# Padding the k tiles of hT by 16 bytes in a one-core decoder layer

## The chip, the cores and the metric

The kernel runs on one NeuronCore of one Trainium2 chip. The metric is the device time of one execution in microseconds; lower is better. All numbers below are of the kernel before the change.

## What is computed

One hybrid decoder layer on 256 tokens with a model width of 2048, all in float32:

```python
h = _rms_norm(x, attn_norm_g[l])
proj = h @ w_in[l]
da_q, da_k, da_v, r_q, r_k, r_v, r_g, m_q, gates = _split_cols(proj, IN_SIZES)
o_da = _diff_attention(...)
o_ret = _retention(...)
o_mem = _memory_attention(...)
merged = (sigmoid(g_da) * (o_da @ w_o_da[l])
          + sigmoid(g_ret) * (o_ret @ w_o_ret[l])
          + sigmoid(g_mem) * (o_mem @ w_o_mem[l]))
x = x + merged @ w_out[l]
hf = _rms_norm(x, ffn_norm_g[l])
x = x + (silu(hf @ w_ffn_gate[l]) * (hf @ w_ffn_up[l])) @ w_ffn_down[l]
```

`w_in` is 2048 x 13312, `mem` has 256 tokens and its own 2048 x 2048 weights, `w_ffn_gate` and `w_ffn_up` are 2048 x 5632, `w_ffn_down` is 5632 x 2048. Almost all of the work is matrix products of 256 tokens with these weights.

## The kernel before, in words

**Products.** A product of activations and weights is made of matmuls of 128 x 128 stationary elements with 512 streamed columns. The stationary operand, the one that is loaded into the array ahead of each matmul, is a tile of transposed activations; the streamed operand is a piece of the model's weights. (In the profile "PEld" is the load of the stationary tile and "PE" the matmul; "weights" in this text and in the change's name are the model's weights, which are streamed.) Both are kept as two parts of the type float32r, a high part and the rest, and a product is three matmuls into one PSUM bank: high x high, high x rest, rest x high (`three_passes`, lines 1592 to 1600, and `product`, lines 1688 to 1692). So in each group of three the stationary tile is hi, hi, lo.

**The activations.** `hT_hi` and `hT_lo` (lines 137 and 138) hold the transposed activations: 128 partitions, KD = 16 tiles for the 16 pieces of 128 of the model width, and TOK = 256 tokens in each tile, that is 1024 bytes per partition and tile. A matmul takes one half of a tile (tokens 0 to 127 or 128 to 255, 512 bytes). They hold the normalised x for the input projection and all three branch gates, later the normalised residual for the feed-forward part, and at the end four tiles of the last feed-forward activations. `oT_hi` and `oT_lo` hold other activations in the same form (the memory tokens, the branches' outputs, the merged columns), `aT_hi` and `aT_lo` those of the down projection. `r_cmb`, `p_cmb` and `cmb` hold sums and differences of blocks of hT (`combine`, line 1424; also lines 1066 and 1313): in part of the products, seven block products are made in place of eight, and four of these take a block of hT and three a combined one.

**Places in SBUF.** Tensors are allocated one behind the other. The small constants come first, then a filler of 32 bytes (`align`, line 136), hT_hi, hT_lo, and behind them everything large: `raw`, `w_hi`, `w_lo` (a ring of four pieces of weights, as loaded, high part and rest), the mixers' tensors and, over the same space, the feed-forward part's. The sizes of all these large ones are multiples of 512 bytes per partition.

**Order of the work.** Stages in order of time: the memory's keys and values on oT (8.6 to 96 us), the memory queries on hT (to 140), the plain and the combined part of the input projection on hT (to about 411), the differential attention and the retention with the gates on hT and the output projections on oT (to about 840), the output projection on oT (to 935), the first feed-forward tile on hT (to 973), ten feed-forward steps with gate and up on hT and combined tiles and down on aT (to 1590), and the last down projection on hT (to 1621). Each engine runs its own program, written out by hand in this order. SyncE's queue brings the model's weights in pieces of 512 KB; ScalarE makes the high part of each piece and VectorE the rest; TensorE waits on `lo_done` (or `part_lo` in the feed-forward part) and releases the slot with `pair_used` (or `part_done`). Between the matmuls on weights stand the small ones of the three attentions and groups of transposes (`turn`, line 1622), four to eight at a time.

**What writes and reads hT besides matmuls.** ScalarE writes hT_hi tile by tile from the transposed input (`high_input`, line 535) and later from PSUM (`high_columns`, line 541), VectorE writes hT_lo in the same way (lines 964 and 956), and at the end one operation of each engine writes four tiles (lines 824 and 1422). VectorE adds hT_hi and hT_lo to make the combined tiles (lines 1066, 1313 and 1427).

Of the kernel before, what the change touches and what calls it, by code (L numbers as in the profile page):

```python
# [27 lines left out]
F32R = mybir.dt.float32r  # L28
# [5 lines left out]
P = 128  # L34
D = 2048
TB = 2
TOK = TB * P
NCOL = 512
KD = D // P
# [52 lines left out]
def program(nc, x, mem, positions, w_in, da_q_norm_g, da_k_norm_g, da_lambda_q1, da_lambda_k1,  # L92
# [6 lines left out]
    with ExitStack() as ctx:  # L99
        def sb(name, shape, dt=F32):  # L100
            return ctx.enter_context(nc.sbuf_tensor(name, shape, dt))
# [32 lines left out]
        rden = sb("rden", [P, 4, 2])  # L134
        lrden = sb("lrden", [P, 2, 2])
        sb("align", [P, ALIGN])
        hT_hi = sb("hT_hi", [P, KD, TOK], F32R)
        hT_lo = sb("hT_lo", [P, KD, TOK], F32R)


        with ExitStack() as mixers:
# [1918 lines left out]
```

## Time and profile before

| | |
|---|---|
| median of two runs | 1623.25 us (1622.8 to 1623.7) |
| the profiled execution, its own time | 1622.59 us |
| its span in the trace | 1620.8 us |
| instructions in the trace | 19825 |
| matmuls | 7355 |
| TensorE matmuls busy | 1613.9 us |
| VectorE, ScalarE, GpSimd busy | 1305.7, 915.7, 80.6 us |
| transfers | 341.45 MB, on average 211 GB/s |

The span is what lies between the first and the last record of the trace; the execution's own time is 1.8 us more. A busy TensorE is not TensorE at its peak: matmuls overlap in the pipe, and the trace models their ends. Starts are records, so the distance of two starts is what to look at.

### The profile page before, as it was taken

What the parts mean: (1) busy time and instruction counts of PE and PEld (TensorE: products, weight loads), DVE (VectorE), ACT (ScalarE), POOL (GpSimd) and SP (SyncE); (2) the same over time, 40 slices, a digit from 0 to 9 for tenths busy, and PEclk for the clock granted to TensorE, in tenths of its full rate; (3) what the DMA queues carried; (4) which work ended last, traced back from release to release, by engine and by line L of the source; (5) the groups of instructions that cost most, each with busy time, mean ns of one, the idle gap of its engine ahead of it and who ended that gap; (6) DMA issues with size and microseconds to landing.
All of it is one profiled execution on the core that took longest, in us unless ns stands there. A gap on an engine that the chain in (4) does not pass through costs nothing.

```text
span 1620.8 us, 19825 instructions
## 1 busy us (share of the span) xinstructions
PE 1613.9 (100%) x7355; PEld 1336.1 (82%) x7355; DVE 1305.7 (81%) x1361; ACT 915.7 (56%) x993; POOL 80.6 (5%) x73
## 2 busy tenths in 40 slices
PE   9999999999999999999999999999999999999999
PEld 7888888888888888888888888888888888888887
DVE  5565658898677777787975589999999999999995
ACT  6654555555555544444554455665656655656653
POOL 0000000000011000000000000100100100100101
PEclk9999999999999999999999999999999999999999
DMA  9776555666645555566666746868868868868866
GB/s 351 268 214 194 157 150 177 213 201 196 193 156 168 165 162 172 180 186 202 206 233 192 258 147 210 256 211 254 243 216 245 252 206 251 246 217 240 251 213 177
DMA packets 178013, 341.45 MB, mean 211 GB/s; under 512 B 11792, under 2 KB 16400, under 8 KB 177168
## 3 DMA queue, kind: packets, MB, share of 16 engines
q1 hardware_dynamic: 167056, 319.45, 60.8%
q0 software_dynamic: 10880, 20.97, 7.1%
q8 instruction: 49, 0.80, 0.2%
q14 instruction: 28, 0.23, 0.0%
HBM read 317.31 MB, written 2.10 MB: 197 GB/s over the span
## 4 chain that ended last, share of the span: by engine, by line
PE 85%; issue 11%; DVE 1%; POOL 1%; DMA 1%; ACT 0%; DVEq 0%; ACTq 0%; SPq 0%; POOLq 0%
PE acc L1600 38%; PE at L1692 9%; PE at L1691 9%; PE at L1690 9%; PE acc L1692 5%; PE acc L1690 5%; PE acc L1691 5%; PE at L1600 3%; PE at L1622 2%; POOL rstd L487 1%; PE at L1653 0%; PE at L1670 0%; DMA raw<-in_w_mem_kv 0%; DMA raw<-in_w_in 0%; DVE w_lo L938 0%
## 5 line engine op out<-in xcount | busy, mean ns | idle before, releaser
L938 DVE TENSOR_TENSOR w_lo<-raw,w_hi 128x1024 fp32r<-128x1024 f32 x313 | 378.9, 1223 | 196.0 <-ACT w_hi L514 190.7
L514 ACT ACTIVATE w_hi<-raw 128x1024 fp32r<-128x1024 f32 x313 | 330.6, 1060 | 341.9 <-PE acc L1600 274.0
L1600 PE MATMUL acc<-w_hi,hT_hi 128*128 128x512 f32 x664 | 262.8, 396 | 0.0
L1600 PE MATMUL acc<-w_hi,hT_lo 128*128 128x512 f32 x664 | 258.8, 390 | 0.0
L1600 PE MATMUL acc<-w_lo,hT_hi 128*128 128x512 f32 x664 | 258.6, 390 | 0.0
L866 ACT ACTIVATE f_hi<-sum 128x2048 fp32r<-128x2048 f32 x60 | 115.3, 1922 | 122.0 <-DVE sum L1479 118.8
L1600 PE MATMUL acc<-w_hi,oT_hi 128*128 128x512 f32 x384 | 151.2, 394 | 1.1 <-DVE oT_lo L964 1.1
L1600 PE MATMUL acc<-w_hi,oT_lo 128*128 128x512 f32 x384 | 149.7, 390 | 0.0
L1600 PE MATMUL acc<-w_lo,oT_hi 128*128 128x512 f32 x384 | 149.4, 389 | 0.0
L1445 DVE TENSOR_TENSOR f_raw_rest<-f_raw,f_hi 128x2048 fp32r<-128x2048 f32 x64 | 145.3, 2284 | 4.3 <-ACT f_hi L856 4.3
L1600 PEld LDWEIGHTS acc<-w_hi,hT_hi 128*128 128x128 f32 x664 | 124.7, 188 | 27.4 <-issue 1.3
L1600 PEld LDWEIGHTS acc<-w_hi,hT_lo 128*128 128x128 f32 x664 | 124.6, 188 | 26.6
L1600 PEld LDWEIGHTS acc<-w_lo,hT_hi 128*128 128x128 f32 x664 | 124.8, 188 | 25.0
L1458 DVE TENSOR_TENSOR sum_rest<-sum,f_hi 128x2048 fp32r<-128x2048 f32 x60 | 137.2, 2287 | 3.9 <-ACT f_hi L866 3.9
L1690 PE MATMUL at<-f_hi,aT_hi 128*128 128x512 f32 x320 | 124.7, 390 | 0.0
L1692 PE MATMUL at<-f_hi,aT_lo 128*128 128x512 f32 x320 | 124.6, 389 | 0.0
L1691 PE MATMUL at<-f_raw_rest,aT_hi 128*128 128x512 f32 x320 | 124.5, 389 | 0.0
L856 ACT ACTIVATE f_hi<-f_raw 128x2048 fp32r<-128x2048 f32 x64 | 119.8, 1904 | 0.0
L1690 PE MATMUL acc<-f_hi,hT_hi 128*128 128x512 f32 x280 | 109.9, 392 | 0.0
L1692 PE MATMUL acc<-f_hi,hT_lo 128*128 128x512 f32 x280 | 109.0, 389 | 0.0
L1452 DVE TENSOR_TENSOR f_raw_rest<-f_raw,f_hi 128x1536 fp32r<-128x1536 f32 x60 | 105.2, 1754 | 0.7
L861 ACT ACTIVATE f_hi<-f_raw 128x1536 fp32r<-128x1536 f32 x60 | 88.9, 1482 | 11.8 <-PE acc L1692 9.4
(348 smaller groups left out, 2858.6 us busy)
## 6 DMA issues: line engine op xcount, KB each, us to landing
raw<-in_w_in SPq DMA_DIRECT2D x208, 512.0 KB, 3.8
f_raw<-in_w_ffn_down SPq DMA_DIRECT2D x88, 512.0 KB, 5.0
f_raw<-in_w_ffn_gate SPq DMA_DIRECT2D x80, 512.0 KB, 4.0
f_raw<-in_w_ffn_up SPq DMA_DIRECT2D x80, 512.0 KB, 5.2
proj<-down POOLq DMA_DIRECT2D x40, 512.0 KB, 6.5
raw<-in_w_mem_kv SPq DMA_DIRECT2D x32, 512.0 KB, 5.7
raw<-in_w_out SPq DMA_DIRECT2D x32, 512.0 KB, 3.9
raw<-in_w_o_mem SPq DMA_DIRECT2D x16, 512.0 KB, 5.0
```

The costliest lines, as they stand in the source:

```text
L514: act.activation(w_hi[:, s % RING], raw[:, s % RING], ACT.Copy).then_inc(hi_done, 1)
L856: act.activation(f_hi[slot(f, p)][:], f_raw[unit(f, u) % RAWS][:], ACT.Copy).then_inc(part_hi, 1)
L861: act.activation(f_hi[slot(f, p)][:, 0:3], f_raw[unit(f, u) % RAWS][:, 1:4], ACT.Copy).then_inc(part_hi, 1)
L866: act.activation(f_hi[slot(f, p)][:], sums[sum_buf(f, i)][:], ACT.Copy).then_inc(part_hi, 1)
L938: v.tensor_tensor(w_lo[:, s % RING], raw[:, s % RING], w_hi[:, s % RING].bitcast(F32), ALU.subtract).then_inc(lo_done, 1)
L1445: v.tensor_tensor(f_rest[r][:], f_raw[r][:], f_hi[slot(f, p)][:].bitcast(F32), ALU.subtract).then_inc(part_lo, 1)
L1452: v.tensor_tensor(f_rest[r][:, 1:4], f_raw[r][:, 1:4], f_hi[slot(f, p)][:, 0:3].bitcast(F32), ALU.subtract).then_inc(part_lo, 1)
L1458: v.tensor_tensor(sums_rest[n][:], sums[n][:], f_hi[slot(f, p)][:].bitcast(F32), ALU.subtract).then_inc(part_lo, 1)
L1600: e = pe.matmul(dst, a[:, k0 + k, tok], w[:, s % RING, k, :], start=first and k == 0 and n == 0, stop=last and k == 1 and n == 2)
L1690: pe.matmul(dst, hi, whi, start=first, stop=False)
L1691: pe.matmul(dst, hi, wlo, start=False, stop=False)
L1692: return pe.matmul(dst, lo, whi, start=False, stop=last)
```

## The change

Each of the two tensors gets 260 elements per tile in place of 256 and is then cut back to the first 256 of each, so that all code behind it stays as it is. Tile k begins at 1040 k bytes from the tensor's start where it began at 1024 k. Each tensor grows by 256 bytes per partition. With the second one starting 256 bytes later, its tiles fall between those of the first modulo 512, and the 2 x 16 tiles have 32 different distances, in steps of 16 bytes, from any place in the weights' buffers. The sum of 512 bytes leaves all later tensors where they were modulo 512.

```diff
@@ -134,8 +134,8 @@
         rden = sb("rden", [P, 4, 2])
         lrden = sb("lrden", [P, 2, 2])
         sb("align", [P, ALIGN])
-        hT_hi = sb("hT_hi", [P, KD, TOK], F32R)
-        hT_lo = sb("hT_lo", [P, KD, TOK], F32R)
+        hT_hi = sb("hT_hi", [P, KD, TOK + 4], F32R)[:, :, 0:TOK]
+        hT_lo = sb("hT_lo", [P, KD, TOK + 4], F32R)[:, :, 0:TOK]
 
 
         with ExitStack() as mixers:
```

## Rows read from the trace of the kernel before

**Rows 1.** The page's head: span, busy time by engine, TensorE's clock in 40 slices.

```profile
span 1620.8 us, 19825 instructions
...
PE 1613.9 (100%) x7355; PEld 1336.1 (82%) x7355; DVE 1305.7 (81%) x1361; ACT 915.7 (56%) x993; POOL 80.6 (5%) x73
...
PEclk9999999999999999999999999999999999999999
```

**Rows 2.** Waits of TensorE: total us, times, longest us.

```profile
PE at L1622 <- POOL ident L471: 2.0, 1, 2.0
PE acc L1600 <- DVE oT_lo L964: 1.1, 1, 1.1
```

**Rows 3.** Busy time by stretch, feed-forward part: us, PE, PEld, DVE, ACT, POOL, clock, DMA.

```profile
973.00:1590.00 617.00, 617.00 (x2767) 510.92 (x2766) 583.58 (x436) 380.13 (x297) 45.36 (x38) 1.00 0.78 235
```

**Rows 4.** The chain in order of time, first feed-forward tile: start us, us, what.

```profile
935.14 38.10 PE acc L1600 x168
```

**Rows 5.** Groups by form: busy us, mean ns of one, idle before.

```profile
L1600 PE MATMUL acc<-w_hi,hT_hi 128*128 128x512 f32 x664 | 262.8, 396 | 0.0
...
L1690 PE MATMUL at<-f_hi,aT_hi 128*128 128x512 f32 x320 | 124.7, 390 | 0.0
...
L1691 PE MATMUL at<-sum_rest,cmb_hi 128*128 128x512 f32 x180 | 70.0, 389 | 0.0
...
L1600 PEld LDWEIGHTS acc<-w_lo,hT_hi 128*128 128x128 f32 x664 | 124.8, 188 | 25.0
```

**Rows 6.** Busy time of what touches hT_hi, then hT_lo: PE, PEld, DVE (ACT).

```profile
17.00:1621.00 1604.00, 727.93 (x2346) 437.17 (x2346) 23.82 (x43) 14.39 (x33) 1.00 0.68 210
...
0.00:1621.00 1621.00, 456.89 (x1173) 220.18 (x1173) 23.82 (x43) 1.00 0.68 211
```

**Rows 7.** Timeline of the loads of stationary tiles, retention stage: start us, us.

```profile
701.02 0.19 PEld L1600 LDWEIGHTS acc<-w_hi,oT_lo 128*128 128x128 f32 x1
...
703.84 0.19 PEld L1600 LDWEIGHTS acc<-w_hi,oT_hi 128*128 128x128 f32 x1
703.95 0.19 PEld L1600 LDWEIGHTS acc<-w_lo,oT_hi 128*128 128x128 f32 x1
```

**Rows 8.** Timeline of the matmuls there: start us, us; four transposes at 703.51.

```profile
700.56 0.39 PE L1600 MATMUL acc<-w_hi,oT_lo 128*128 128x512 f32 x1
...
701.02 0.39 PE L1600 MATMUL acc<-w_lo,oT_hi 128*128 128x512 f32 x1
...
703.28 0.39 PE L1600 MATMUL acc<-w_hi,oT_lo 128*128 128x512 f32 x1
...
704.18 0.40 PE L1600 MATMUL acc<-w_lo,oT_hi 128*128 128x512 f32 x1
...
704.65 0.40 PE L1600 MATMUL acc<-w_hi,oT_hi 128*128 128x512 f32 x1
704.89 0.39 PE L1600 MATMUL acc<-w_lo,oT_hi 128*128 128x512 f32 x1
705.11 0.39 PE L1600 MATMUL acc<-w_hi,oT_lo 128*128 128x512 f32 x1
...
706.27 0.39 PE L1600 MATMUL acc<-w_lo,oT_hi 128*128 128x512 f32 x1
```

**Rows 9.** Element-wise operations on hT: ns min/median/max, first and last start.

```profile
L541 ACT ACTIVATE hT_hi<-at,g_cols x16: 456/472/484, 868.2 to 936.4; 128x256 fp32r<-128x256 f32 x16
L824 ACT ACTIVATE hT_hi<-acc x1: 1025/1025/1025, 1590.3 to 1590.3; 128x1024 fp32r<-128x1024 f32 x1
...
L956 DVE SCALAR_TENSOR_TENSOR hT_lo<-at,g_cols,hT_hi x16: 473/474/478, 869.5 to 937.8; 128x256 fp32r<-128x256 f32 x16
...
L1427 DVE TENSOR_TENSOR sum<-hT_hi,hT_lo x2: 1219/1752/2285, 942.9 to 949.2; 128x2048 f32<-128x2048 f32 x1, 128x1024 f32<-128x1024 f32 x1
L1422 DVE TENSOR_TENSOR hT_lo<-acc,hT_hi x1: 1225/1225/1225, 1591.4 to 1591.4; 128x1024 fp32r<-128x1024 f32 x1
```

## The prediction

> **What bounds the kernel now.** I read the page's head first: TensorE's matmuls are busy 1613.9 of 1620.8 us, at the full granted clock (1.00, so the 2.4 GHz level) in every slice; weight loads are busy 82%, VectorE 81%, ScalarE 56% [rows 1]. Then I asked who makes TensorE wait. Its waits on another engine come to 2.0 and 1.1 us, both in the first 9 us [rows 2]. In the feed-forward part, where VectorE is busiest (583.6 of 617 us), TensorE still has no gap at all (617.0 of 617.0) [rows 3]. So everything outside TensorE is cover, and the time is the number of matmuls times their pitch, the distance from one start to the next. The "mean ns of one" in the groups is not that pitch: 389 to 396 ns [rows 5] is how long one is in the pipe, and they overlap. The chain of work gives the pitch: 168 matmuls on hT in 38.10 us are 226.8 ns each [rows 4].
>
> What a pitch is made of matters here. At 2.4 GHz, 512 columns take 213.3 ns. So some 13.5 ns of each 226.8 are something else, and this is the only thing that the placement of hT in SBUF could touch. The time in the pipe hardly differs between hT, aT and the combined tiles (389 and 390 ns; 396 in a group with many first matmuls after a break) [rows 5].
>
> **The change part by part.** hT_hi and hT_lo get a row pitch of 260 elements in place of 256, so tile k begins at 1040 k bytes and not 1024 k. Nothing is issued more or less: the same 7355 matmuls, transfers and element-wise operations of the same sizes.
>
> *Where things lie.* Before, all tiles of hT, their second halves (512 bytes on) and all later tensors are whole multiples of 512 bytes apart. After it, hT_hi's tile k is 16 k bytes off (0 to 240), hT_lo starts 16 x 16 = 256 bytes later and covers 256 to 496: these are the 32 distances. The two tensors grow by 512 bytes together, so raw, w_hi, w_lo and all behind them keep their place modulo 512. Only the stationary operand of the matmuls on hT moves against the streamed weights; oT, aT and the combined tiles don't.
>
> *How many matmuls.* 2346 matmuls of the trace read hT_hi and 1173 read hT_lo [rows 6], that is 3519. At 226.8 ns they are 798 us, half the span. Each nanosecond of pitch on them is 3.5 us, and 2% of the time (32.5 us, about what a measurement of this kernel can tell from no change) is 9.2 ns on each of them.
>
> *What does the load of hT cost a matmul?* The load of the next tile begins within 10 ns of the start of the matmul it hides behind (701.02 both [rows 7, 8]), and takes 0.19 us (188 ns in the groups [rows 5]) of a pitch of 0.227, so it ends before it is needed. Two loads with nothing between them stand 0.11 us apart (703.84 and 703.95) [rows 7]: reading a tile of 512 bytes per partition takes about 110 ns, and in that time the matmul beside it streams 0.11 / 0.227 of its 2048 bytes, some 990. The stream therefore gains 480 bytes on the load, about one lap of 512. If the two disturb each other where their addresses agree modulo 512, they meet about once per load wherever they start; the distance says when, not how often. The same holds for any smaller period. By this the pitch stays at 226.8, and the edit costs 0.
>
> *The bounds of that.* Right after a break the pitch is not settled. Before the four transposes of this stretch, twelve steps from 700.56 to 703.28 take 2.72 us, 226.7 ns each; behind them, nine steps from 704.18 to 706.27 take 2.09 us, 232 ns each, with single steps between 0.22 (704.89 to 705.11) and 0.24 (704.65 to 704.89) [rows 8]. After that it is 227 again. So there is some state that outlasts an instruction, and it settles when all matmuls are alike. Every second or third load of hT would now step to another distance (hi, hi, lo: 256 bytes on and back, and 16 at each k). If that keeps the state unsettled, hT's matmuls cost 232 and not 226.8: 3519 x 5.4 = +19 us; with the combined tiles' matmuls that stand among them in the feed-forward part (180 in the group of [rows 5], of six passes in all: three of 180 and three of 60, 720), +23. At the longest step, 240 ns, on all: 3519 x 13.2 = +46 us. On the other side, the shortest step, 0.22 (some 224 ns), on all would be -10 us, and 213.3 on all, which no row shows, 3519 x 13.5 = -47 us. I take 0, the row it is nearest to: the pitch stays at 226.8 over 168 matmuls in a row [rows 4], whose operands lie at many different multiples of 512 from each other.
>
> The Trainium skill ("TensorE: Matmul & The Clock Gate", "Back-to-back issue gap") speaks against taking 226.8 as a floor: it gives about N/2.4 + 2.5 ns, 215.8 for 512 columns. This trace doesn't agree, it shows 11 ns more; were these 11 a clash on hT alone that goes away, an estimate from that page would be 3519 x 11 = 39 us less.
>
> *Element-wise work on hT.* ScalarE writes hT_hi tile by tile (twice 16 operations, 0.47 us in the second set), VectorE hT_lo likewise (0.47 us) [rows 9]; they are contiguous still, only off by multiples of 16 bytes. VectorE's additions that read several tiles have gaps to cross now (the longest 2.3 us), and near the end one operation of each engine writes four tiles at once (1.0 and 1.2 us) [rows 9]. All work on hT and hT_lo is 23.8 us of VectorE and 14.4 of ScalarE [rows 6]. If each took twice as long, these sums would be added once more, spread over the run, and TensorE has its own work beside them: the second sets lie between 868 and 938 us. So I cost it at nothing; without cover the dearest piece is the pair near 1590 us, 2.2 us.
>
> *Sum.* Profiled execution 1622.6 us (span 1620.8 and 1.8 around it), plus 0: 1622.6; the two timed runs of before have their median 0.7 higher, 1623.25. Forecast 1623.0.
>
> **The rivals.**
> *Unsettled pitch (slower).* Mechanism and price as above: the distance changes from load to load, the start-up pattern of rows 8 never dies out, +19 us (1642), +23 with the neighbours (1646). For it: the pattern exists and has a fixed length, which looks like two streams falling into step. Against it: it follows transposes and other matmuls of another kind whatever the tile, and may be only the queue filling again. It decides from 9.2 ns of mean pitch, 236 ns, on being slower by 2%. A load that must touch one more block of memory because its tile isn't aligned any more would cost on the same matmuls, and its size would fall within the same bounds.
> *Clash goes away (faster).* The 13.5 ns are a clash that hT has at distance 0 modulo 512, and at most other distances it has not. At all of it -47 us (1576); at a quarter, which is about the shortest step seen, -12 (1611). For it: 13.5 ns are unexplained. Against it: the lap argument, and loads that aren't longer beside a stream than the groups' 188 ns.
> *Element-wise operations come on the path.* Near the end and where hT is turned for the feed-forward part, at most a few us: 1625. Cover speaks against it.
>
> **How the numbers follow.** No effect of the distance 0.52 (with the element-wise case, 0.05 of it: 1622 to 1626). Slower by 4 to 32 us 0.22, by more 0.08. Faster by 3 to 32 us 0.10, by more 0.08. The forecast is the likeliest, 1623.0. The range goes down to the shortest step seen on all of hT's matmuls (1611) and up to the unsettled pitch with its neighbours (1646); beyond lie the two tails and a part of the middle cases. Faster by over 2%: 0.08, within 2%: 0.84, slower by over 2%: 0.08.
>
> **What would show it right or wrong.** Right: after the change, long stretches of matmuls on hT in the chain still give 226.7 ns (38.1 us for the 168 near 935 us), and oT's and aT's too. Unsettled: hT's stretches at about 232 with single steps of 0.22 to 0.24, while aT's stretches, which don't touch hT, stay at 226.7. Clash gone: hT's below 226. Element-wise: new entries among TensorE's waits. The forecast is wrong if the settled pitch depends on where the stationary tile starts modulo a few tens of bytes; I have no row with such a tile to exclude it.

## The result: 15.5 us slower, all of it in the pitch of the matmuls

| | before | after |
|---|---|---|
| median of two runs | 1623.25 us | 1638.79 us (1638.78 to 1638.80) |
| ratio | | 1.0097, 95% interval 1.0080 to 1.0113 |
| span of the profiled execution | 1620.8 us | 1637.0 us |

The forecast was no change, 1623.0. The 1638.8 lie inside the range that it gave, 1611 to 1646, but the kernel is slower clear of the noise, and the forecast had it the same: it was wrong. The page's head of the kernel after, as [rows 1]:

```profile
span 1637.0 us, 19825 instructions
...
PE 1629.9 (100%) x7355; PEld 1336.6 (82%) x7355; DVE 1306.5 (80%) x1361; ACT 916.6 (56%) x993; POOL 80.6 (5%) x73
...
PEclk9999999999999999999999999999999999999999
```

The same instructions, the same clock, the other engines busy as long as before; the matmuls' busy time is up by 16.0 us and the span by 16.2. TensorE waits 0.2 us more than before. Its waits (total us, times, longest), as [rows 2]:

```profile
PE at L1622 <- POOL ident L471: 2.0, 1, 2.0
PE acc L1600 <- DVE oT_lo L964: 1.3, 1, 1.3
```

So almost nothing is late; the matmuls themselves stand further apart. The chain of the kernel after (start us, us, what), a stretch on oT and then the first feed-forward tile on hT, as [rows 4]:

```profile
853.13 19.06 PE acc L1600 x84
873.06 21.81 PE acc L1600 x96
...
943.88 38.89 PE acc L1600 x168
```

On hT 38.89 / 168 = 231.5 ns where it was 226.8. On oT, whose tiles didn't move against the streamed weights, 19.06 / 84 = 226.9 (the 21.81 us for 96, 227.2 ns each, begin behind a break). The timeline of the kernel after shows tile by tile where it starts. These are the last matmuls on oT and the first on hT, in the order of tiles 0, 1, 2 with six matmuls each (hi, hi, lo for either half of the tokens):

```profile
95.91 0.39 PE L1600 MATMUL acc<-w_hi,oT_lo 128*128 128x512 f32 x1
96.13 0.39 PE L1600 MATMUL acc<-w_hi,hT_hi 128*128 128x512 f32 x1
...
97.49 0.39 PE L1600 MATMUL acc<-w_hi,hT_hi 128*128 128x512 f32 x1
...
98.63 0.40 PE L1600 MATMUL acc<-w_hi,hT_lo 128*128 128x512 f32 x1
98.86 0.39 PE L1600 MATMUL acc<-w_hi,hT_hi 128*128 128x512 f32 x1
99.09 0.39 PE L1600 MATMUL acc<-w_lo,hT_hi 128*128 128x512 f32 x1
99.32 0.40 PE L1600 MATMUL acc<-w_hi,hT_lo 128*128 128x512 f32 x1
99.56 0.40 PE L1600 MATMUL acc<-w_hi,hT_hi 128*128 128x512 f32 x1
...
101.88 0.40 PE L1600 MATMUL acc<-w_lo,hT_hi 128*128 128x512 f32 x1
```

Tile 0 begins at 96.13, tile 1 at 97.49, tile 2 at 98.86. From 96.13 to 98.63, 11 steps, take 2.50 us: 227, the settled pitch. The 14 steps from 98.63 to 101.88 take 3.25 us: 232. The first slow one is the last matmul of tile 1: beside it runs the load of tile 2's high part, the first tile at a distance of 32. Tiles at 0, 16, 256 and 272 bytes did nothing. The single starts say the same of the end of the pass: tile 15 (240 and 496) is at 226.7 again, in both whole passes of the memory queries.

Where the 16.2 us are, from the single starts of both traces, against a pitch of 226.67: matmuls on hT +14.7, on the combined tiles +1.8, on oT +0.7, on aT +0.2, together 17.4; the breaks with transposes and attention matmuls are 1.2 shorter. Element-wise work on hT is unchanged: VectorE's longest addition over the gaps is still 2.3 us and its write of four tiles 1.2, as in [rows 9] (operation, count, ns min/median/max):

```profile
L1427 DVE TENSOR_TENSOR sum<-hT_hi,hT_lo x2: 1219/1752/2286, 951.8 to 958.0; 128x2048 f32<-128x2048 f32 x1, 128x1024 f32<-128x1024 f32 x1
L1422 DVE TENSOR_TENSOR hT_lo<-acc,hT_hi x1: 1225/1225/1225, 1607.2 to 1607.2; 128x1024 fp32r<-128x1024 f32 x1
```

### The profile page after: what moved, and what is told of

Same layout as the page of the kernel before. It is cut to its first block, busy times and chain, and to the rows that moved or that the text cites. A ratio compares the mean times of both kernels' runs of the same rounds, so it can differ in the third digit from the quotient of the medians.

```text
span 1637.0 us, 19825 instructions
## 1 busy us (share of the span) xinstructions
PE 1629.9 (100%) x7355; PEld 1336.6 (82%) x7355; DVE 1306.5 (80%) x1361; ACT 916.6 (56%) x993; POOL 80.6 (5%) x73
## 4 chain that ended last, share of the span: by engine, by line
PE 99%; DMA 0%; DVE 0%; SPq 0%; ACT 0%; issue 0%
PE acc L1600 44%; PE at L1692 9%; PE at L1691 9%; PE at L1690 9%; PE at L1600 6%; PE acc L1690 6%; PE acc L1692 6%; PE acc L1691 6%; PE at L1622 2%; PE at L1653 0%; PE at L1670 0%; DMA raw<-in_w_mem_kv 0%; PE at L1763 0%; PE at L1761 0%; PE acc L1622 0%; PE at L1802 0%
```

## The experiments

Three theories stood after the result. *Distance*: a load disturbs the stream beside it for some distances of its tile from the streamed piece and not for others. *Change*: what unsettles the pitch is that the distance changes from load to load, as the prediction's rival had it. *Alignment*: a tile that doesn't start at a multiple of 64 bytes costs.

### The distances one by one

A kernel with nothing but matmuls of the layer's form, one segment of 24 to 36 for each place, the two output tensors `even` and `odd` taking turns so that the timeline shows segments apart:

```diff
+            for i, (pattern, s, count) in enumerate(SEG):
+                for n in range(count):
+                    d = 4 * pattern[n % len(pattern)]
+                    e = pe.matmul(ps[i % 2][:], a[:, d:d + P], w[:, 4 * s:4 * s + 512], start=n == 0, stop=n == count - 1)
```

> A kernel of matmuls alone (same form as the layer's: 128x128 stationary, 512 streamed columns, float32r), all else left out: the output is not the layer's. Segments of 24 to 36 matmuls, each at one place of the stationary tile: 32 constant distances in steps of 16 bytes; 16 segments in which both operands move together by 16-byte steps; 31 in which only the streamed piece moves; 7 with alternating distances; 36 distances in steps of 4 bytes. Theory 'distance' (the load of a tile disturbs the matmul beside it when the tile lies 32 to 224 bytes modulo 256 from the streamed piece): segments at distance 0, 16, 240, 256, 272 and 496 settle at 226.7 ns, the others stay at 229 to 236 for all their matmuls, and moving both together changes nothing. Rival 'change' (only a change of distance from load to load unsettles the pitch): every constant distance goes back to 226.7 within ten matmuls, and only the alternating segments stay at 230 or more. Rival 'alignment' (a tile that doesn't start at a multiple of 64 bytes costs): 3 of 4 constant distances and 3 of 4 of the common shifts are slow, and distances 64, 128 and 192 are not.

The timeline of this kernel (start us, us, what): first distances 0, 16, 32 and 48, then 176, 192 and 208, then 240 to 304, then the first segment of the next series (distance 0 again), then four patterns: (0, 0, 256), (0, 0, 128), (128, 128, 384), (0, 16):

```profile
19.41 6.96 PE L73 MATMUL even<-w,a 128*128 128x512 f32 x30
26.21 6.97 PE L73 MATMUL odd<-w,a 128*128 128x512 f32 x30
33.02 7.15 PE L73 MATMUL even<-w,a 128*128 128x512 f32 x30
40.01 7.16 PE L73 MATMUL odd<-w,a 128*128 128x512 f32 x30
...
95.98 7.06 PE L73 MATMUL odd<-w,a 128*128 128x512 f32 x30
102.88 7.04 PE L73 MATMUL even<-w,a 128*128 128x512 f32 x30
109.77 7.16 PE L73 MATMUL odd<-w,a 128*128 128x512 f32 x30
...
123.75 6.96 PE L73 MATMUL odd<-w,a 128*128 128x512 f32 x30
130.55 6.96 PE L73 MATMUL even<-w,a 128*128 128x512 f32 x30
137.35 6.97 PE L73 MATMUL odd<-w,a 128*128 128x512 f32 x30
144.16 7.15 PE L73 MATMUL even<-w,a 128*128 128x512 f32 x30
151.15 7.16 PE L73 MATMUL odd<-w,a 128*128 128x512 f32 x30
...
241.69 5.60 PE L73 MATMUL even<-w,a 128*128 128x512 f32 x24
...
502.34 8.36 PE L73 MATMUL odd<-w,a 128*128 128x512 f32 x36
510.54 8.49 PE L73 MATMUL even<-w,a 128*128 128x512 f32 x36
518.87 8.54 PE L73 MATMUL odd<-w,a 128*128 128x512 f32 x36
527.24 8.44 PE L73 MATMUL even<-w,a 128*128 128x512 f32 x36
```

Read the starts: at distance 0 and 16, 6.80 and 6.81 us for 30 matmuls, 226.7 and 227 ns; at 32, 6.99, 233.0. At 176 6.90 (230.0), at 192 6.89 (229.7), at 240, 256 and 272 again 6.80, 6.80 and 6.81, at 288 6.99. The first 16 distances take 130.55 - 19.41 = 111.14 us, the next 16 241.69 - 130.55 = 111.14: the period is 256 bytes, and the mean is 231.5 ns (111.14 / 480), as on the 168 matmuls on hT in the changed kernel. Tile by tile the two agree as well: in a pass of the memory queries the six steps of tile 5 (80 bytes) average 230.5 ns, of tile 6 (96 bytes) 233.7, of tile 11 (176 bytes) 229.5 and of tile 15 (240 bytes) 226.7, and in the bare kernel these distances have 231.9, 234.3, 229.9 and 226.7. The constant distances don't go back to 226.7; in the single starts a distance of 128 alternates 229 and 238 to its end, one of 64 231 and 236. So *change* falls as the condition, since constant distances are slow without any change, and *alignment* too: 16 and 240 are not multiples of 64 and cost nothing here, 64 and 128 are and cost 6.7 ns.

The patterns: (0, 0, 128), one load in three at a bad distance, is 8.33 / 36 = 231.4, and the single starts settle at 231.1, two thirds of the way from 226.7 to the 233.3 of 128 alone. The pattern (0, 16) shows that a change of distance can cost too: 527.24 to 535.51 are 8.27 us for 36, and the steps settle at 230.0, while either distance alone gave 226.7. In the segments where both operands move together the distance is 0; the even steps (32-byte steps) settle at 226.7, the odd ones at 230.0 in the single starts. So the streamed piece's own place counts as well, by 3.3 ns. I had expected nothing of that. The 31 segments in which only the streamed piece moves say it once more. Moved by 256 bytes it gives 226.7 again, and moved by other multiples of 32 bytes it gives the pitch of the same distance reached by the tile (only 128 settles at 232.4 and not at 233.3); moved by odd multiples of 16 it often doesn't: distance 240 is 231.7 there, not 226.7. So distance alone fixes the pitch only while the streamed piece stays where it is, as in the change. Distances in 4-byte steps settle anywhere from 226.7 (at 120 and 132 bytes) to 235 (at 28).

### In the layer: the second tensor 256 bytes on, and all of hT 128 bytes on

```diff
         hT_hi = sb("hT_hi", [P, KD, TOK], F32R)
+        sb("between", [P, 64])
         hT_lo = sb("hT_lo", [P, KD, TOK], F32R)
+        sb("behind", [P, 64])
```

> The kernel before with hT_lo 256 bytes further from hT_hi and all else at its place modulo 512: stationary tiles at two distances, 0 and 256, alternating hi, hi, lo. Theory 'distance' with period 256: nothing changes, 1623 us. Theory 'distance' with period 512, or rival 'change': hT's pitch no longer settles, 230 to 232 ns on 3519 matmuls, 1635 to 1642 us. Rival 'alignment': 1623 us.

Measured 1622.91 us against 1622.81 before, ratio 1.0000 (0.9989 to 1.0012). The period of 256 holds in the layer, and changing between distances 0 and 256 from load to load costs nothing. For other pairs of good distances that isn't shown: (0, 16) cost 3.3 ns in the bare kernel.

```diff
+        sb("ahead", [P, 32])
         hT_hi = sb("hT_hi", [P, KD, TOK], F32R)
         hT_lo = sb("hT_lo", [P, KD, TOK], F32R)
+        sb("behind", [P, 96])
```

> The kernel before with hT_hi and hT_lo both 128 bytes further from the weights' buffers, tiles 1024 bytes apart as before: one distance, 128, for all of hT, aligned to 64. Theory 'distance': all 3519 matmuls on hT are disturbed, 231 ns or more, 1638 us or above (the changed kernel had 26 of 32 tiles so). Rival 'change' and rival 'alignment': the pitch settles as before, 1623 to 1625 us.

Measured 1644.17 us, ratio 1.0129 (1.0100 to 1.0159), +21.4 us. The chain of this kernel at the first feed-forward tile:

```profile
945.92 39.03 PE acc L1602 x168
```

39.03 / 168 = 232.3 ns. Here the tiles are 1024 bytes apart as before, all aligned, all alike, and it is slower than the changed kernel. This one run refutes both rivals as the cause: nothing changes from load to load and nothing is misaligned.

### How large is the load's part, and does the past count

> Matmuls alone again (all else of the layer left out). (1) 24 matmuls each with a stationary tile of 128, 96, 64 and 32 columns at distance 0, 128, 64 and 32. If the 13.3 ns above 512 columns at 2.4 GHz are the load of the next tile getting in the way of the stream, the pitch falls with the columns: at distance 0 near 223, 220 and 217 ns, and at distance 128 the 20 ns of extra fall to about 15, 10 and 5. If they are a fixed cost of a matmul, the pitch stays at 226.7. (2) Shorter streams of 448, 384, 320 and 256 columns beside a whole load: the extra stays the same in ns while the load fits beside the stream. (3) Breaks of four 128-column matmuls, then 20 at one distance: at 0 the unsettled steps of the layer (up to ten), at 16 and 240 fewer. (4) 24 matmuls at another distance (0, 48, 128 or 192), then 24 at 0, 16 or 240: one settled pitch for each distance, or two that depend on what came before (16 gave 226.7 once and 233.3 once).

The series with smaller stationary tiles, from the timeline: 128, 96, 64 and 32 columns at distance 0, then the same at 128:

```profile
19.32 5.61 PE L66 MATMUL even<-w,a 128*128 128x512 f32 x24
24.77 5.69 PE L66 MATMUL odd<-w,a 128*96 128x512 f32 x24
30.29 5.68 PE L66 MATMUL even<-w,a 128*64 128x512 f32 x24
35.80 5.72 PE L66 MATMUL odd<-w,a 128*32 128x512 f32 x24
41.37 5.74 PE L66 MATMUL even<-w,a 128*128 128x512 f32 x24
46.94 5.72 PE L66 MATMUL odd<-w,a 128*96 128x512 f32 x24
52.51 5.67 PE L66 MATMUL even<-w,a 128*64 128x512 f32 x24
58.01 5.71 PE L66 MATMUL odd<-w,a 128*32 128x512 f32 x24
63.56 5.76 PE L66 MATMUL even<-w,a 128*128 128x512 f32 x24
```

By the starts 227.1, 230.0, 229.6 and 232.1 ns at distance 0, and 232.1, 232.1, 229.2 and 231.3 at 128. The loads do get shorter, 188, 161, 135 and 108 ns (means of a load), but a quarter of the load doesn't cost less; at distance 0 it costs more. The expectation that the price goes with the columns was a miss. Shorter streams at distance 0 settle, in the single starts, at 206.7, 173.3, 146.7 and 120.0 ns for 448, 384, 320 and 256 columns; with 226.7 for 512 all are whole multiples of 6.67 ns, 13.3 above the columns at 2.4 GHz but for 448, which is 20 above. (512 less 256 columns are 106.7 ns, 0.417 ns a column, one cycle at 2.4 GHz.) At distance 128 the pitch settles at 118.6 for 256 columns and 204.0 for 448, below distance 0, at 146.7 for 320, the same, and at 176.0 for 384, above it. That the extra stays the same in ns was a miss too, and 0 is not the best distance for every shape.

After breaks of four short matmuls, distance 0 and 256 go back to 226.7 within ten steps each time, distance 16 stays at 233.3 each time, and 240 ends once at 226.7 and twice at 228.3. Entered from long runs at 0, 48 or 192, distance 16 stays at 226.7, from 128 at 233.3. Distance 16 thus has two settled pitches, and what came before picks one. Distance 128 has two as well: 232.4 in most segments of this kernel and 233.3 in one.

### Distance 16 and distance 240 in the layer

```diff
-        hT_hi = sb("hT_hi", [P, KD, TOK], F32R)
-        hT_lo = sb("hT_lo", [P, KD, TOK], F32R)
+        def hT_at(name, room, ahead):
+            return sb(name, [P, KD * TOK + room], F32R)[:, ahead:ahead + KD * TOK].rearrange("p (k c) -> p k c", k=KD)
+
+        hT_hi = hT_at("hT_hi", 8, 4)
+        hT_lo = hT_at("hT_lo", 120, 60)
```

> The kernel before with hT_hi at distance 16 and hT_lo at 272 from the weights' buffers, tiles 1024 bytes apart, nothing else moved modulo 512. Theory 'distance': settled at 226.7 as before, 1623 us; after a break it settles on another number of steps, worth at most some 5 us either way, and it may lock at 233.3 after some breaks (up to +20 us). Rival 'alignment to 64': every load of hT misaligned, 1635 us or more.

Measured 1630.46 us, ratio 1.0043 (1.0026 to 1.0060), +7.8. Both settled pitches stand in one trace, in two stretches of the chain:

```profile
290.61 10.88 PE at L1603 x48
...
940.39 39.20 PE acc L1603 x168
```

10.88 / 48 = 226.7 ns in the input projection, 39.20 / 168 = 233.3 in the first feed-forward tile. With `hT_at("hT_hi", 64, 60)` and `hT_at("hT_lo", 64, 60)`, distance 240:

> The same with hT_hi at distance 240 and hT_lo at 496. Theory 'distance': settled at 226.7; entering from other distances took one or two steps there in the row of m1_distances (234, 227, 226) where distance 0 took up to ten, so 2 to 6 us faster than before, 1617 to 1621 us. If the steps after a break have another cause than the place of the tile: 1623 us. Rival 'alignment to 64': 1635 us or more.

Measured 1623.63 us, ratio 1.0004 (0.9995 to 1.0014). No difference shows; the gain of 2 to 6 us that I expected from a shorter way back after breaks was a miss.

### One tensor at a time

The two halves of the change, each with a filler behind so that nothing else moves modulo 512:

```diff
-        hT_hi = sb("hT_hi", [P, KD, TOK], F32R)
+        hT_hi = sb("hT_hi", [P, KD, TOK + 4], F32R)[:, :, 0:TOK]
         hT_lo = sb("hT_lo", [P, KD, TOK], F32R)
+        sb("behind", [P, 64])
```

> One part of the change: hT_hi's tiles 1040 bytes apart, hT_lo's 1024 as before, all of them at distance 256. Two of three loads of hT (hi, hi, lo) change their distance. Theory 'sum' (each load costs by its own distance alone): two thirds of the change's 15.5 us, +10.4, 1633 us. Theory 'memory' (a disturbed load also spoils the next matmuls, up to ten after it): nearly all of it, +13 to +15, 1636 to 1638 us.

> The other part: hT_lo's tiles 1040 bytes apart, at 0 to 240; hT_hi's at 0 as before. One of three loads of hT changes its distance. Theory 'sum': +5.2 us, 1628 us. Theory 'memory': in m1_distances one load in three at distance 128 gave 231.1 ns where all at 128 gave 233.3 and none 226.7, two thirds of the whole; so +9 to +12 us, 1632 to 1635 us.

The first gave 1637.43 us against 1623.57 (ratio 1.0088, 1.0071 to 1.0105), +13.9; the second, with the padding on hT_lo, 1634.90 (1.0069, 1.0052 to 1.0085), +11.3. Their sum, 25.2, is far above the whole, 15.5. The same 168 matmuls in the chain of the kernel with only hT_hi padded, then of that with only hT_lo padded:

```profile
943.32 38.85 PE acc L1601 x168
```

```profile
943.04 38.72 PE acc L1601 x168
```

231.3 and 230.5 ns. With only one load in three moved, four fifths of the 4.7 ns are there. A disturbed load spoils the matmuls after it too. The kernel with only hT_lo padded shows it on tile 2, whose part in hT_lo is the first at distance 32, while all of hT_hi is at 0:

```profile
100.07 0.39 PE L1601 MATMUL acc<-w_hi,hT_hi 128*128 128x512 f32 x1
100.29 0.40 PE L1601 MATMUL acc<-w_lo,hT_hi 128*128 128x512 f32 x1
100.53 0.39 PE L1601 MATMUL acc<-w_hi,hT_lo 128*128 128x512 f32 x1
100.76 0.40 PE L1601 MATMUL acc<-w_hi,hT_hi 128*128 128x512 f32 x1
100.99 0.40 PE L1601 MATMUL acc<-w_lo,hT_hi 128*128 128x512 f32 x1
101.23 0.39 PE L1601 MATMUL acc<-w_hi,hT_lo 128*128 128x512 f32 x1
```

In whole nanoseconds the steps are 227, 235, 228, 233 and 239. The load of the hT_lo tile runs beside the second of these matmuls, which gets 235. The step of 233 from 100.76 has its own tile and the load beside it at distance 0, and is slow all the same. The pitch takes up to ten matmuls to settle, and with the order hi, hi, lo a bad load comes every third. Part of the excess of the halves may be another thing: with one tensor padded the distance modulo 256 changes between hi and lo, with both padded it is the same for all six matmuls of a tile. No run tells the two shares apart.

### The same with bfloat16

> Matmuls alone with both operands in bfloat16 (tile 256 bytes, stream 1024 bytes per partition; all else of the layer left out): 32 distances in steps of 16 bytes, then 4 segments at distance negative by 16 to 64. If the disturbance is one of 4-byte operands, the pitch is flat near 216 ns whatever the distance; if it is a matter of any load beside any stream, some distances cost 3 to 7 ns as they do in float32r.

The first three of 36 segments of the timeline (the counts of 23 are missing records):

```profile
17.63 5.34 PE L65 MATMUL even<-w,a 128*128 128x512 bf16 x23
22.81 5.34 PE L65 MATMUL odd<-w,a 128*128 128x512 bf16 x24
27.99 5.34 PE L65 MATMUL even<-w,a 128*128 128x512 bf16 x23
```

Every segment is 5.18 us for 24 matmuls, 215.8 ns, at all distances. This is the 215.8 of the formula N/2.4 + 2.5 ns in the Trainium skill ("TensorE: Matmul & The Clock Gate", "Back-to-back issue gap"): the trace agrees for bfloat16, and for float32r the formula's figure isn't reached at any distance tried. The same section also gives about 131 ns per matmul of 512 columns for a stream of loads and matmuls; no run here shows that.

## Why the prediction was wrong

- *What bounds the kernel* held: no new wait, and everything outside TensorE stayed cover. So did the count of 3519 matmuls, 3.5 us for each nanosecond on them, the places modulo 512 and the element-wise work at nothing.
- *What does the load of hT cost a matmul* is the step that failed. It said that load and stream meet about once per load wherever they start, so the distance decides when and not how often, and that "the same holds for any smaller period". The runs show a pitch that depends on the distance with a period of 256 bytes: 226.7 at 0, 228.9 to 234.3 at 32 to 224. What they also show is a rhythm: the settled steps repeat after a few matmuls, and each repeat lasts a whole number of 6.67 ns, 34 a matmul at distance 0, on the mean 35 a matmul at most others, 103 for three at 192, 246 for seven at 96. My reading, which no run shows, is that counting meetings left out that a stall moves the stream against the next load.
- *I take 0, the row it is nearest to* leaned on 168 matmuls in a row at 226.8 whose operands lie at many multiples of 512 from each other. Those rows had one distance modulo 256 only. They could say nothing of another, and the last sentence of the prediction came near to saying so. A chance of 0.52 for no effect was too much on rows that never varied the quantity in question. Nor did 2% bound what could be told from no change: 0.97% was clear of the noise, with an interval of 0.8 to 1.13%.
- The rival *unsettled pitch* gave the right sign and place and nearly the size, +19 to 1642 against 1638.8: hT at 232 expected and 231.5 measured, steps of 0.22 to 0.24, oT's and aT's stretches hardly touched, the neighbours with combined tiles slower too (+1.8 us where it had 4). Its mechanism was half right. That a state outlasts an instruction and spreads to neighbours is shown by the half changes. That the distance must change from load to load for it is refuted: all of hT at 128 costs 21.4 us, more than the 32 distances. The size agrees because the unsettled steps after a break and the settled steps at a bad distance are both between 224 and 241; that they average alike is luck. Modulo 256 the high part and the rest of a tile have the same distance even after the change, so the step "256 bytes on and back" on which the rival rested is none, and the distance changes only every sixth matmul.
- The size by the cause: mean over 32 distances 231.5 less 226.8, times 3519, is +16.5 us. The matmuls on hT account for 14.7 of the 16.2 us between the spans: the steps that aren't settled after a break made their mean 227.1 before the change, and it is 231.4 after it (gaps at the breaks themselves left out). The neighbours with combined tiles add 1.8. So the close agreement of 16.5 with 16.2 is partly chance.
- *Clash goes away* is out for this shape: of all distances none settled below 226.7. The 13.5 ns above 213.3 are there with a quarter of the load as well, so no placing tried removes them; what they are isn't shown. There is a slip beside it: the shortest step on all of hT is -10 us, 1613, by the prediction's own working, and the range began at 1611. Nothing hangs on it.

What stays open is which part of the memory or of TensorE makes the rhythm. That the distance decides with a period of 256 bytes, that what ran before can pick between two rhythms, and that these go by 6.67 ns, is measured; why, isn't.

## What to carry to other kernels

In a kernel bound by float32r matmuls, the place of the stationary tile against the streamed piece is a term of its own, 3% of a 512-column matmul: for 512 columns keep both at the same address modulo 256, and check the pitch in the chain before anything else when a tensor in front changes its size. In the bare kernel both moved together had to move by multiples of 32 bytes; no run in the layer moved the streamed pieces. For 256 and 448 columns distance 128 was a little faster than 0. Spreading tiles over addresses is no cure here, since it averages over good and bad places and the bad ones spoil their neighbours. To learn whether a quantity matters, look for rows in which it varies; if there are none, a kernel of bare matmuls tells it in one run.

## What I had not expected of the hardware

- float32r, 512 columns, 2.4 GHz: 226.7 ns at best, up to 235 settled by the tile's place alone (240 with a tile of 32 columns), period 256 bytes. bfloat16: 215.8 at every distance.
- One distance can have two or more settled pitches: 16 bytes gave 226.7 and 233.3, chosen by what ran before, 128 bytes 232.4 and 233.3, 240 bytes 226.7 and 228.3.
- The settled pitches at distance 0 are whole multiples of 6.67 ns for 256 to 512 columns, and at other distances the repeating groups of steps are.
- Both operands moved together by an odd multiple of 16 bytes: 230.0 instead of 226.7.
- The load's own time hardly shows any of it: 187 to 192 ns for a load at every distance in 16-byte steps. The disturbed one is the stream, so the groups' mean of a weight load is no place to look for this.
